# Applying the first norm's factor at the projections' eviction, and loading x in feature groups

## What is computed

```python
def rms_norm(x, g):
    xf = x.astype(jnp.float32)
    y = xf * lax.rsqrt(jnp.mean(xf * xf, axis=-1, keepdims=True) + NORM_EPS)
    return (y * g.astype(jnp.float32)).astype(x.dtype)
...
        hn = rms_norm(h, pre_norm_g[l])
        proj = hn @ w_in[l]
        q, kv6, gates, z_a, feat_b, z_b = jnp.split(proj, [o1, o2, o3, o4, o5], axis=-1)
```

## Time and profile before

| | us |
|---|---|
| three runs | 3187.07, 3189.02, 3192.75 |
| their median | 3189.02 |
| the profiled execution, its own time | 3188.98 |
| its span, first to last instruction | 3187.2 |
| PE busy | 3144.7 (99%) |
| DVE busy | 1769.4 (56%) |
| ACT busy | 1254.5 (39%) |
| first projection product starts | 24.16 |
| last product of `start` starts | 48.83 |
| first product of `nsa` starts | 50.47 |

### The profile page before, as it was taken

The page is one execution under the profiler, slowest core; times in us unless marked ns, Lnnn a source line. Parts: engine busy times, 40 slices in busy tenths (PEclk is TensorE's granted clock), DMA queues, the critical chain, the costliest instruction groups (busy, mean ns, idle before and its releaser), DMA issues. The chain is left out here.

```text
span 3187.2 us, 51639 instructions
## 1 busy us (share of the span) xinstructions
PE 3144.7 (99%) x21539; PEld 2570.3 (81%) x21539; DVE 1769.4 (56%) x3074; ACT 1254.5 (39%) x1992; POOL 185.4 (6%) x148
## 2 busy tenths in 40 slices
PE   8999999999999999999999999999999999999999
PEld 6877777777778778678888888888888888888787
DVE  5235555565666653644457775335556655665822
ACT  4124343433444422423346665333344434443421
POOL 0000000001010101000001010110000000000000
PEclk9999999999999999999999999999999999999999
DMA  8433333333232443333331213533223323332452
GB/s 247 115 77 93 90 93 96 97 90 87 62 96 70 151 140 94 115 95 103 102 103 53 60 50 119 152 111 110 87 83 96 93 74 99 93 93 80 159 159 79
DMA packets 492526, 324.25 MB, mean 102 GB/s; under 512 B 27130, under 2 KB 448605, under 8 KB 491782
## 3 DMA queue, kind: packets, MB, share of 16 engines
q1 hardware_dynamic: 492294, 320.94, 34.7%
HBM read 276.05 MB, written 44.85 MB: 101 GB/s over the span
## 5 line engine op out<-in xcount | busy, mean ns | idle before, releaser
L535 PE MATMUL PS<-XH,WHT 128*128 128x512 f32 (+1 forms) x2224 | 899.9, 405 | 2.9 <-DVE AR L1032 1.2
L523 DVE TENSOR_TENSOR WLT<-AR,WHT 128x1024 fp32r<-128x1024 f32 (+1 forms) x430 | 526.5, 1230 | 657.3 <-ACT WHT L517 656.8
L537 PE MATMUL PS<-XH,WLT 128*128 128x512 f32 (+1 forms) x2224 | 872.5, 392 | 0.0
L517 ACT ACTIVATE WHT<-AR 128x1024 fp32r<-128x1024 f32 (+1 forms) x430 | 446.9, 1042 | 632.6 <-PE PS L537 473.4
L536 PE MATMUL PS<-XL,WHT 128*128 128x512 f32 (+1 forms) x1712 | 670.1, 391 | 0.0
L535 PEld LDWEIGHTS PS<-XH,WHT 128*128 128x128 f32 (+1 forms) x2224 | 416.7, 187 | 105.3 <-issue 11.3
L537 PEld LDWEIGHTS PS<-XH,WLT 128*128 128x128 f32 (+1 forms) x2224 | 416.9, 187 | 98.1
L536 PE MATMUL PS<-ARR,WHT 128*128 128x512 f32 x1024 | 404.4, 395 | 0.0
L536 PEld LDWEIGHTS PS<-XL,WHT 128*128 128x128 f32 (+1 forms) x1712 | 320.9, 187 | 71.8 <-issue 4.8
L536 PEld LDWEIGHTS PS<-ARR,WHT 128*128 128x128 f32 x1024 | 192.4, 188 | 40.1 <-issue 0.2
L535 PE MATMUL PS<-XL,WHT 128*128 128x512 f32 x512 | 203.4, 397 | 0.1
(11 more groups left out here) (492 smaller groups left out, 5126.8 us busy)
## 6 DMA issues: line engine op xcount, KB each, us to landing
AR<-b_w_in SPq DMA_DIRECT2D x128, 512.0 KB, 4.0
AR<-w_in SPq DMA_DIRECT2D x122, 512.0 KB, 4.1
AR<-a_w_in SPq DMA_DIRECT2D x48, 512.0 KB, 4.3
AR<-w_out SPq DMA_DIRECT2D x32, 512.0 KB, 4.4
AR<-a_w_out SPq DMA_DIRECT2D x32, 512.0 KB, 4.0
AR<-b_w_out SPq DMA_DIRECT2D x32, 512.0 KB, 4.0
proj_scratch<-AR SPq DMA_DIRECT2D x33, 256.0 KB, 2.3
AR<-a_w_kv_up SPq DMA_DIRECT2D x32, 256.0 KB, 4.0
```

The costliest lines, as they stand in the source:

```text
L517: self.nc.scalar.activation(self.shaped(self.high, n), self.shaped(self.raw, n), ACT.Copy).then_inc(self.s_high, 1)
L523: self.nc.vector.tensor_tensor(self.shaped(self.low, n), self.shaped(self.raw, n), f32(self.shaped(self.high, n)), ALU.subtract).then_inc( ...
L535: mm(out, wh, xh[k0 + c], start=(start and c == 0), stop=False)
L537: last = mm(out, wl, xh[k0 + c], start=False, stop=(stop and c == nk - 1))
```

## The change

The norm's factor is no longer multiplied into the inputs of the first projections. `XH` and `XL` hold x times gain alone; the factor, one number per token, is kept in a buffer (`FACTOR`) and multiplied into every projection tile as it leaves its bank. Since `start`'s products need only the gain, they begin before any sum of squares.

- x is loaded in four feature groups of 512 features (all tokens), with weight units 0 and 1 after the first group and 2 and 3 after the third. The gain is loaded from ACT's queue.
- PE turns four feature blocks before the products, then one ahead of each of the products' blocks 1 to 12. High and low parts are made from the bank (ACT, DVE), and the copies into `RES` go from the same bank, even blocks on ACT and odd on DVE.
- Sums of squares move behind the high parts of blocks 9, 11, 13 and 15; the spread of the factor follows all products.
- The store of the residual is four DMAs, each followed by one weight unit's load. The evictions of `nsa` wait for all four, as before for the one.
- Gate tiles: DVE multiplies by the factor into SBUF, ACT takes the sigmoid of that into a buffer `SG`, and a further DVE multiply (`gated`) joins them later.

The diff, cut to its core:

```diff
+def layer1_factor(k):
+    return k.EXT[:, 0, :]
...
+            def columns(g):
+                sp.dma_start(X[:, :, g * NCOL:(g + 1) * NCOL], d["x"][0, :, g * NCOL:(g + 1) * NCOL].rearrange("(b p) n -> p b n", p=P)).then_inc(x_in[g], 16)
...
-            for b in range(TB):
-                sp.dma_start(X[:, b, :], d["x"][0, b * P:(b + 1) * P, :]).then_inc(x_in[b], 16)
+            columns(0)
+            st.load(sp, 0)
+            st.load(sp, 1)
+            columns(1)
+            columns(2)
+            st.load(sp, 2)
+            st.load(sp, 3)
+            columns(3)
...
-            sp.dma_start(k.RESD.rearrange("c p t -> p c t"), k.RES[:, :, :]).then_inc(res_out, 16)
-            for u in range(4, 8):
-                st.load(sp, u)
+            for g in range(TB):
+                copied(sp, 4 * g + 2)
+                copied(sp, 4 * g + 3)
+                sp.dma_start(k.RESD[4 * g:4 * g + 4, :, :].rearrange("c p t -> p c t"), k.RES[:, 4 * g:4 * g + 4, :]).then_inc(res_out, 16)
+                st.load(sp, 4 + g)
...
+            def turn(c):
+                if c % 4 == 0:
+                    pe.wait_ge(x_in[c // 4], 16)
+                if c >= 4:
+                    copied(pe, c - 4)
+                for b in range(TB):
+                    last = nc.tensor.transpose(TURN[c % 4][:, b * P:(b + 1) * P], X[:, b, c * P:(c + 1) * P], C("ident"))
+                last.then_inc(turned, 1)
+            def ready(c):
+                if c and c + 3 < KT:
+                    turn(c + 3)
+                pe.wait_ge(low, c + 1)
...
+            act.wait_ge(g_c, 1)
+            for c in range(KT):
                 to_high(c)
-                if c in (3, 5):
-                    st.split_high(act, (c + 1) // 2)
+                if c == 0:
+                    st.split_high(act, 0)
+                    st.split_high(act, 1)
+                if c in (5, 7):
+                    st.split_high(act, 2 + (5, 7).index(c))
+                if c % 2:
+                    copy(c - 1)
+                if c in (9, 11, 13, 15):
+                    square((c - 9) // 2)
             st.split_high(act, 4)
             st.split_high(act, 5)
...
+            for c in range(KT):
+                to_low(c)
+                if c % 2:
+                    dve.wait_ge(low, c + 1)
+                    V.tensor_copy(k.RES[:, c, :], TURN[c % 4][:, :]).then_inc(d_copied, 1)
+                if c == 0:
+                    st.split_low(dve, 0)
+                    st.split_low(dve, 1)
+                if c in (5, 7):
+                    st.split_low(dve, 2 + (5, 7).index(c))
+                if c in (11, 13, 15):
+                    factor((c - 11) // 2)
+            factor(TB - 1)
+            st.split_low(dve, 4)
             dve.wait_ge(spread, TB)
+            V.tensor_copy(layer1_factor(k), RSB[:, :])
             st.split_low(dve, 5)
...
-                V.tensor_copy(out, bank).then_inc(evac_d, 1)
+                TTn(out, bank, FACTOR, ALU.mult).then_inc(evac_d, 1)
...
-            dve.wait_ge(res_out, 16)
+            dve.wait_ge(res_out, 16 * TB)
...
             def sigmoid(t):
-                if t is None or tiles[t][0] != "zb":
+                if t not in sigmoids:
                     return
-                m = t - first
-                act.wait_ge(st.s_used, 2 * t + 2)
-                if m >= 2:
-                    act.wait_ge(s_store[m % 2], 16 * (m // 2))
-                A(EV[:, m % 2, :], B[FBK][:, :], ACT.Sigmoid).then_inc(a_sig, 1)
+                act.wait_ge(evac_d, t - first + 1)
+                act.wait_ge(z_gated, sigmoids.index(t))
+                A(SG, EV[:, (t - first) % 2, :], ACT.Sigmoid).then_inc(a_sig, 1)
...
-                ev, bank = EV[:, m % 2, :], B[FBK][:, :]
-                if tiles[t][0] == "zb":
-                    dve.wait_ge(a_sig, sigmoids.index(t) + 1)
-                    TTn(ev, bank, ev, ALU.mult).then_inc(evac_d, 1)
-                else:
-                    if m >= 2:
-                        dve.wait_ge(s_store[m % 2], 16 * (m // 2))
-                    V.tensor_copy(ev, bank).then_inc(evac_d, 1)
+                if m >= 2:
+                    dve.wait_ge(s_store[m % 2], 16 * (m // 2))
+                TTn(EV[:, m % 2, :], B[FBK][:, :], FACTOR, ALU.mult).then_inc(evac_d, 1)
+            def gated(t):
+                if t not in sigmoids:
+                    return
+                ev = EV[:, (t - first) % 2, :]
+                dve.wait_ge(a_sig, sigmoids.index(t) + 1)
+                TTn(ev, ev, SG, ALU.mult).then_inc(z_gated, 1)
```

More of the change, by code:

```diff
@@ L321, in start, with copied @@
     g_t, g_c, r_t = k.sem("gain_turned"), k.sem("gain_copied"), k.sem("rows_turned")
[L322 to L328, removed]
-        else:
[L330 to L336, removed]
+    high, low = k.sem("first_hi"), k.sem("first_lo")
+    def copied(eng, c):
+        eng.wait_ge((d_copied, a_copied)[c % 2 == 0], c // 2 + 1)
     with k.block() as block:
@@ L365, in _ @@
         def _(pe):
-            pe.wait_ge(small, 16)
[L367 to L374, removed]
-            pe.wait_ge(g_in, 16)
-            nc.tensor.transpose(ROWB[:, 0:NG1], rows[0:NG1, 0, :], C("ident")[0:NG1, 0:NG1]).then_inc(g_t, 1)
+            def turn(c):
[10 more added lines that the diff above has]
+                pe.wait_ge(low, c + 1)
+            pe.wait_ge(small, 16)
+            pe.wait_ge(g_in, 16)
+            nc.tensor.transpose(ROWB[:, 0:NG1], gain[0:NG1, :], C("ident")[0:NG1, 0:NG1]).then_inc(g_t, 1)
+            for c in range(4):
+                turn(c)
+            st.pair(pe, (0, 1), PAIR, k.XHT, k.XLT, 0, True, False, ready)
+            st.pair(pe, (2, 3), PAIR, k.XHT, k.XLT, 8, False, True, ready)
             for b in range(TB):
@@ L544, in pair @@
         mm = self.nc.tensor.matmul
-        for n in units:
-            pe.wait_ge(self.s_low, n + 1)
         for c in range(nk):
@@ L1325, in _ @@
                     store(u // 2 - 1)
-            store(first + PRE - 1)
             for i in range(NPAIR):
@@ L1332, in _ @@
                         st.load(sp, unit(i, j) + 4)
-                    if j == 0 and i and late(i - 1) is not None:
+                    if j == 1 and late(i - 1) is not None:
                         store(late(i - 1))
@@ L1814, in _ @@
             ahead(7)
-            sigmoid(first + 3)
             for i in range(NPAIR):
@@ L1833, in _ @@
                         gates(i + 1, 0)
-                    if l == 3:
+                    if l == 1:
+                        sigmoid(late(i - 1))
+                    if l == 4:
                         sigmoid(early(i))
@@ L1862, in _ @@
                     token_major(i + 1, B_, "B")
-                sigmoid(late(i))
                 if more:
```

150 lines of the change are left out of this document (70 added, 80 removed).

## The result

The changed kernel takes 3204.29 us (median of five runs, 3202.50 to 3206.20) against 3189.02 (3187.07 to 3192.75): ratio 1.0047, 95% interval 1.0032 to 1.0062. It is 15.3 us slower, where 3188.4 was forecast with a range up to 3194.5. The profiled execution has 3206.20 us, its span is 3204.4; times between the two traces differ by 17.2 at the end. Single executions of the experiments fell in a slower state (one of 3467 us, one of 5143); ratios and their intervals leave them out.

A forecast was written before the change was run, and what follows sets the result against it. PE, busy 99% of the span, was taken as the bound, so only its waits count. Restart -2.1, half clock +2.0 and evictions -0.4 gave -0.5 against 3188.98: 3188.4 us, range 3183.0 to 3194.5.

The forecast's parts named there:

- Part 3: Attention and recurrence: multiplying at evictions costs nothing, the gates' extra 11 us of DVE is covered, banks free sooner: -0.4 us.
- Part 1: Start: products begin earlier, block 1 near 13.3 us, and PE's last product ends about 9 us earlier, near 40.
- the aside on the constants: Change of block: constants issued at 24.0 alone, with the smaller clock loss, would give 3186.7 us.
- Part 2: Change of block: what is late next; restart 2.1 us earlier, with 2.0 us lost again to the half clock.
- (b): Change of block: the residual's store lands last, at 47.6 us, so PE restarts at 48.35 against 50.47, -2.1.
- (a): End of the start: ACT's and DVE's remaining work ends at 44.1 us, so evictions could begin at 44.5.
- (c): Restart after the change of block: PE's long wait drops its clock to half, costing 1.5 to 2.3 us, +2.0.
- The bank free sooner: Recurrence: DVE no longer waits for ACT's sigmoid, so the projections' bank frees sooner for PE: -0.4 us.
- The gates' chain reaches PE: Recurrence rival: each of 16 gate tiles costs PE 0.69 us, +11 - 0.5, 3199.5 us; chance 0.09.
- The other three rivals: Start and restart: store not last, 3185.4 or 3183.4 (0.12); products' path faster, 3180 (0.06); clock gate's worst, 3190.3 (0.14).
- the two on the restart: Change of block: residual's store not last, restart 45.25 (chance 0.12); store late and clock loss +2.3, 3190.3 (0.14).

The follow-up runs named there:

- the run without the wait: Changed kernel with spill issued before the late tile's store, and DVE not waiting for the residual's store before attention's first eviction: 3183.53 us, ratio 0.9986.
- the wait alone: Kernel before, with SP made to wait in pairs 5 and 6 for the recurrence's second level before issuing the spill: 3202.34 us, ratio 1.0044.
- The first run: Changed kernel with the spill issued ahead of the late tile's store in SP's queue, in all pairs: 3184.63 us, ratio 0.9989.
- the run with one of the two places: Changed kernel with the spill issued ahead of the late tile's store in pair 5 alone: 3194.17 us, ratio 1.0018.

## Why the prediction was wrong

The forecast was 3188.4 us, no difference that can be told; measured were 3204.29 us, a loss of 15.3. The step that failed is the price of the evictions, Part 3.

**Part 1 was right, with one size off.** Block 1 of the products began at 14.29 (13.3 forecast), the last product ended at about 41 (39.4, "up to 1 us more if PE still has the half clock"): it had the half clock from 13.2 to 16.7. (Rounding: the sum gives 3188.5, the aside on the constants 3186.8; nothing hangs on it.)

**Part 2 was right.** (b) The store was last: landed by 46.9 (47.6 forecast), restart 47.74 (48.35), so -2.7 in place of -2.1. The constants were issued at 25.86 (25.2 taken). (a) DVE's tail ended at 45.1 (44.1), and the run without the wait shows that it is next. (c) The clock cost 1.3 to 1.4 of the 2.7 (2.0 forecast), and the run with idle products shows the cause. The size is partly luck: the half clock at this restart lasted 3.4 us here and 6.8 in six other runs with the same start. The start alone measured 0.02% from the kernel before; "no difference" was right for this half.

**Part 3 failed,** and with it the forecast. It put the evictions and gates at -0.4; the run with the evictions alone measured +16.2. Two of its sentences are right. The multiply from the bank costs nothing (692 ns for 691). The bank free sooner is worth about what was taken (-0.4): between 625 and 653 us the traces with the new evictions gain 0.5 and those of the start alone and the wait alone don't; of the changed kernel's further -0.6 up to 890 us the latter two gain as much, so that isn't the evictions'. Which wait of the bank it was, was not followed. The third named the danger as the sigmoid and its table load "between two steps of the recurrence". The traces show them there, and PE waiting for them once, 0.88 us in pair 6. The step that is missing is one on SP's queue: the late tile's store now waits for `z_gated`, an event of the next pair's second level, and the spill stands behind it. The part costed the multiplies, the sigmoid and the bank, and no DMA.

It could have been read from the kernel before. Its store goes out at 990.51, the spill at 996.09, it lands 4.1 us later at 1000.2, and ACT wants the buffer at 1001.53: 1.3 us of slack. The end of the second level, behind which the multiply was put, is this row of DVE:

```profile
1004.93 0.41 DVE L2000 TENSOR_TENSOR AR<-AR,PS 128x256 f32<-128x256 f32 x1
```

That is after ACT's instruction that needs the spill, so the spill could not be in time: 1005.3 and 0.7 for the multiply, then the store, 0.4 and 0.4 for the issues ahead, 4.1 to land: 1010.9, 9.4 late (an estimate from these rows). Measured, ACT came 8.4 late, 1007.41 where it would have been 1001.53 less the 2.5 that the changed kernel was ahead; the spill took 3.0 to land and not 4.1. PE had other work for part of that and waited 5.7 us; this twice, and a fall of the clock at each, as at the start.

**The rivals.** "The gates' chain reaches PE" had the place (the recurrence) and the sign, and a chance of 0.09, but its mechanism is not what happened: its price was 0.69 us on DVE for each of sixteen tiles, the point of decision 0.7 us between PE and DVE, its signature a wait of PE on DVE at the gates' lines. What came are two waits of 5 to 6 us on ACT, released by a DMA, in the two pairs where a gate tile's store and a spill meet. That its 3199.5 lies near the result is an accident. The first run excludes it: the gates' work is all there and the time is 3184.6. The other three rivals ended faster or within 0.2%, and the two on the restart can be read off: the store was last, and the clock did not do its worst.

## What to carry to other kernels

When a step is made to end later, list what stands behind its DMA in the issuing engine's queue, and for each of these who waits for its landing; the wait of a store that nobody hurries for can hold a transfer that the whole chain needs. Give each such transfer its slack from the trace (issue, landing, first use): here it was 1.3 us in one pair and nothing in the next, in a program of 3189. An issue whose event comes late belongs behind those that are ready, or in another engine's queue (here ACT's) where nothing that matters stands behind it.

Where PE must wait a few microseconds, look at its clock behind the wait as well as at the wait: here the wait cost 10.9 us and the half clock behind it another 5.7. At the change of block a few products that nobody reads took that echo away; in the recurrence it was not tried.

## What the runs showed of the hardware

- At the change of block, waits of PE of 1.13 to 1.72 us (1.25 in the kernel before) left the granted clock at 1.00 in five traces; waits of 3.78 to 6.36 us were followed by half clock in eight. After one of 2.64 us the clock was full for the first 1.4 us of work and fell then, for 3.4 us: the price can come behind products that already run at full speed.
- In the recurrence a short wait is not always safe. In the run with PE kept busy, a wait of 1.57 us was followed by 3.4 us at half clock:

```profile
1073.68 0.38 PE L1593 MATMUL PS<-AR 64*64 64x64 f32 x9 [1.57 <-issue]
```

```profile
1075.40:1078.80 3.40, 3.40 (x14) 2.42 (x12) 2.80 (x6) 0.60 (x1) 0.00 (x0) 0.50 0.30 115
```

  The run with unit 5's split moved has the same behind 1.36 us; the kernel before waits 1.64 us near this place and keeps its clock. What decides was not tried.
- The length of the fall does not follow the length of the wait: 6.9 us at half clock around the wait of 5.7, 10.2 around the one of 5.2, and again 6.8 around the same 5.2 in the run with one of the two places. At the change of block it was 6.8 us in six traces, behind waits of 5.3 to 6.4, and 3.4 in the changed kernel, behind 5.41.
- Profiled executions of kernels that differ only after 40 us left the first half clock between 9.5 and 15.6 us (two of them fell back to half once, until 16.3 and 16.7), and PE's work in the start (without the extra products) ended at 40.7 to 42.4 us. At the change to the second layer the half clock lasted 10.2 us in most executions, 13.7 in four and 6.8 in one. A difference of 1 to 2 us between single profiles says nothing here.
